# A mixture-of-experts stage with its first slots split earlier, its first gather by column halves, and its last expert pair and final norm written out

## What is computed

```python
h = h + memory_cross_attention(...)            # its last product is o @ w_xo ("xo1")
hn = rmsnorm(h, norm_ffn_g)
logits = hn @ w_router                         # 8 experts, the top 2 per token
y = zeros
for e in range(8):
    y = y + combine[:, e:e+1] * ((silu(hn @ w_gate[e]) * (hn @ w_up[e])) @ w_down[e])
out = rmsnorm(h + y, norm_final_g)             # D_EXPERT is 3584
```

## Time and profile before

| | us |
|---|---|
| median of three runs | 2310.11 |
| the profiled execution | 2310.16 |
| its span, first to last instruction | 2308.0 |
| PE busy / DVE busy / ACT busy | 2190.6 / 1751.8 / 1330.9 |
| expert stage, first slot's first matmul to its last | 1299.4 to 2288.9 |

### The profile page before, as it was taken

One profiled execution on the slowest core, in us unless ns is written; L12 is line 12 of the kernel. 1 busy time (PEld: TensorE's weight loads), 2 busy tenths in 40 slices (PEclk: granted clock), 3 DMA queues, 4 the chain that ended last, 5 costly groups with the idle time before them and its releaser, 6 DMA issues.

```text
span 2308.0 us, 34771 instructions
## 1 busy us (share of the span) xinstructions
PE 2190.6 (95%) x13807; PEld 1962.3 (85%) x13807; DVE 1751.8 (76%) x1928; ACT 1330.9 (58%) x1306; POOL 76.7 (3%) x160
## 2 busy tenths in 40 slices
PE   7999999999988899999898999999999999999997
PEld 4989988998978899999788888888888788888886
DVE  5768967874885455548865688888898888888887
ACT  3564435553534344435344677777777777777775
POOL 5002200000000000000000000000000000000000
PEclk8998999999999899999999999999999999999998
DMA  9636857655533346556334599999999999999994
GB/s 273 194 124 218 271 177 204 184 175 174 180 118 132 92 133 184 178 164 189 113 128 140 185 359 358 371 334 356 363 367 356 338 371 356 365 335 366 359 371 172
DMA packets 415931, 567.03 MB, mean 246 GB/s; under 512 B 17146, under 2 KB 268260, under 8 KB 415776
## 3 DMA queue, kind: packets, MB, share of 16 engines
q1 hardware_dynamic: 410736, 557.36, 71.3%
q0 software_dynamic: 5040, 7.41, 1.3%
HBM read 562.89 MB, written 1.84 MB: 245 GB/s over the span
## 4 chain that ended last, share of the span: by engine, by line
PE 81%; DVE 9%; ACT 3%; issue 2%; DVEq 0%; ACTq 0%
PE pair L1084 61%; PE misc L1084 13%; DVE arena L2000 3%; DVE wlo L1646 2%; PE misc L1559 1%; PE pair L1526 1%; DVE wlo L2206 1%; ACT whi L638 1%; PE misc L1154 1%; PE misc L1410 1%; PE misc L1138 0%; DVE opl L1664 0%; DVE rt L1671 0%; PE misc L1271 0%; ACT whi L1014 0%
## 5 line engine op out<-in xcount | busy, mean ns | idle before, releaser
L2206 DVE TENSOR_TENSOR wlo<-raw,whi 128x2048 fp32r<-128x2048 f32 x338 | 768.5, 2289 | 113.0 <-ACT whi L1014 111.8
L1014 ACT CAST whi<-raw 128x2048 fp32r<-128x2048 f32 x338 | 646.8, 1917 | 204.0 <-PE pair L1084 120.3
L1084 PE MATMUL pair<-hh,whi 128*128 128x256 f32 x1840 | 533.6, 290 | 23.2 <-DVE hl L1664 19.6
L1646 DVE TENSOR_TENSOR wlo<-raw,whi 128x2048 fp32r<-128x2048 f32 (+1 forms) x174 | 385.0, 2215 | 193.3 <-ACT whi L638 192.6
L1084 PE MATMUL pair<-hl,whi 128*128 128x256 f32 x1840 | 527.6, 287 | 0.0
L1084 PE MATMUL pair<-hh,wlo 128*128 128x256 f32 x1840 | 527.3, 287 | 0.0
L1084 PE MATMUL pair<-whi,oph 128*128 128x512 f32 (+1 forms) x1024 | 391.7, 383 | 5.7 <-DVE wlo L2206 3.9
L1084 PE MATMUL pair<-wlo,oph 128*128 128x512 f32 (+1 forms) x1024 | 386.1, 377 | 0.0
L1084 PE MATMUL pair<-whi,opl 128*128 128x512 f32 (+1 forms) x1024 | 385.9, 377 | 0.0
L1084 PEld LDWEIGHTS pair<-hh,whi 128*128 128x128 f32 x1840 | 360.8, 196 | 29.4 <-issue 25.6
L638 ACT CAST whi<-raw 128x2048 fp32r<-128x2048 f32 (+1 forms) x174 | 320.6, 1843 | 78.8 <-PE pair L1084 71.9
(11 more groups left out here) (437 smaller groups left out, 2480.1 us busy)
## 6 DMA issues: line engine op xcount, KB each, us to landing
raw<-in_moe_w_gate_dram SPq DMA_DIRECT2D x114, 1024.0 KB, 6.9
raw<-in_moe_w_up_dram SPq DMA_DIRECT2D x112, 1024.0 KB, 7.3
raw<-in_moe_w_down_dram SPq DMA_DIRECT2D x112, 1024.0 KB, 6.7
raw<-in_w_in_dram SPq DMA_DIRECT2D x38, 1024.0 KB, 5.7
raw<-in_w_mod_dram SPq DMA_DIRECT2D x24, 1024.0 KB, 5.7
raw<-in_w_up_dram SPq DMA_DIRECT2D x44, 512.0 KB, 5.1
raw<-in_w_xkv_dram SPq DMA_DIRECT2D x16, 1024.0 KB, 5.4
raw<-in_ffn_w_gate_dram SPq DMA_DIRECT2D x22, 512.0 KB, 3.9
```

The costliest lines, as they stand in the source:

```text
L1014: act.copy(whi[:, q, :], raw[:, r, :]).then_inc(sem("hi_ready"), 1)
L1084: ins = pe.matmul(out_, lhs, rhs, start=start and i == 0, stop=stop and i == 2)
L1646: dve.tensor_tensor(wlo[:, i_ % SPLIT, 0:size], raw[:, raw_of(n), 0:size], whi[:, i_ % SPLIT, 0:size].bitcast(F32), ALU.subtract).then_inc ...
L2206: dve.tensor_tensor(wlo[:, q, :], raw[:, r, :], whi[:, q, :].bitcast(F32), ALU.subtract).then_inc(sem("lo_ready"), 1)
```

## The change

- SP no longer loads the two slots of expert 0 at the end of a pass; the second pass loads them itself.
- `moe_hi(0, 0)` and `(0, 1)` stand in ACT's loop over the `xo1` groups, behind the squares of groups 1 and 2; `moe_lo(0, 0)` and `(0, 1)` stand behind DVE's `add_plain` of the same groups.
- The token parts are turned and split in the order 0, 2, 1, 3 (the first column half of both token blocks first). The first gather waits for two parts ahead of banks 0 and 1, and for four ahead of banks 2 and 3.
- The loops over expert pairs have three passes. The last pair follows as straight code, its last expert with `last=True`: no gather, no `placed`, no extra slots; in its last down slot the three products of both row chunks go to column half 0 first and then to half 1, and the output is weighed and split by halves.
- DVE loads the flag ahead of that split. It jumps over the second pass behind it, and only then does the four additions, each with its own signal.
- ACT loads the table of the root ahead of the sums, squares all four parts, sums the two column halves through the bias of the root, and scales token block 0; DVE multiplies block 0 with the gain beforehand and scales block 1.
- Parts are written out in the order 0, 2, 1, 3.

```diff
+LAST_PARTS = (0, 2, 1, 3)
+TOKEN_PARTS = (0, 2, 1, 3)
...
-                for k in (0, 1):
-                    load(NE - 1 + NE * p, 0, k + MOE_SLOTS)
...
+                load(NE, 0, 0)
+                load(NE, 0, 1)
                 moe_pass(1)
-            for q in range(4):
+            for n, q in enumerate(LAST_PARTS):
                 i, cols = q // 2, slice((q % 2) * 512, (q % 2 + 1) * 512)
-                sp.wait_ge(sem("fin_scaled"), q + 1)
+                if i == 0:
+                    sp.wait_ge(sem("x_copied"), 4 + 4 + n // 2 + 1)
+                else:
+                    sp.wait_ge(sem("fin_scaled"), n // 2 + 1)
...
+                if j in (1, 2):
+                    moe_hi(0, j - 1)
...
-            for q in range(4):
-                act.wait_ge(sem("hn_turned"), q + 1)
-                act.activation(hn_hi[:, q // 2, (q % 2) * 512:(q % 2 + 1) * 512], banks[:, q, :], ACT.Copy,
+            for n, q in enumerate(TOKEN_PARTS):
+                act.wait_ge(sem("hn_turned"), n + 1)
+                act.activation(hn_hi[:, q // 2, (q % 2) * 512:(q % 2 + 1) * 512], banks[:, n, :], ACT.Copy,
...
+                if last:
+                    upto(MOE_SLOTS - 1)
+                    act.wait_ge(sem("m_w"), E + 1)
+                    for m in range(2):
+                        if m == 0:
+                            act.wait_ge(sem("ranked"), 2 + p)
+                        else:
+                            act.wait_ge(sem("slot_used"), E * MOE_SLOTS + (n_split + MOE_SLOTS))
+                        act.activation(ye_hi[:, m * 512:(m + 1) * 512], misc[:, 2 + m, :], ACT.Copy, scale=weigh_slot[:])\
+                            .then_inc(sem("m_yc"), 1)
+                    return
...
+                with act.Fori(0, NE // 2 - 1) as i:
                     for u in range(2):
                         moe_expert(i, u, p)
-
-            moe_hi(0, 0)
-            moe_hi(0, 1)
+                for u in range(2):
+                    moe_expert(NE // 2 - 1, u, p, last=u == 1)
...
-            act.wait_ge(sem("moe_added"), 1)
-            act.activation(work[:, 0:4, :].rearrange("p a b -> p (a b)"), x_acc[:, 0], ACT.Square, accum_out=tiny[:, 6, 0:1])\
-                .then_inc(sem("fin_sq"), 1)
-            act.wait_ge(sem("fin_sq"), 2)
-            act.activation(token_root, tiny[:, 6, 0:2], ACT.Sqrt, bias=consts[:, 0:1], scale=1.0 / D).then_inc(sem("root_ready"), 1)
+            act.activation(tiny[:, 7, 2:3], consts[:, 0:1], ACT.Sqrt)
+            for n, q in enumerate(LAST_PARTS):
+                act.wait_ge(sem("moe_added"), n + 1)
+                act.activation(work[:, 2 * n:2 * n + 2, :].rearrange("p a b -> p (a b)"), x_acc[:, q // 2, (q % 2) * 512:(q % 2 + 1) * 512],
+                               ACT.Square, accum_out=tiny[:, 6, n:n + 1]).then_inc(sem("fin_sq"), 1)
+                if n == 1:
+                    act.wait_ge(sem("fin_sq"), 2)
+                    act.activation(tiny[:, 7, 0:2], tiny[:, 6, 0:2], ACT.Identity, bias=consts[:, 0:1], scale=1.0 / D)\
+                        .then_inc(sem("fin_sq"), 1)
+            act.wait_ge(sem("fin_sq"), 5)
+            for i in range(TB):
+                act.activation(token_root[:, i:i + 1], tiny[:, 6, 2 + i:3 + i], ACT.Sqrt, bias=tiny[:, 7, i:i + 1], scale=1.0 / D)\
+                    .then_inc(sem("root_ready"), 1)
+            act.wait_ge(sem("h_scaled"), DC * (NORM["ffn1"] + 1) + 3)
+            for m in range(2):
+                act.activation(x_acc[:, 0, m * 512:(m + 1) * 512], work[:, 4 * m:4 * m + 2, :].rearrange("p a b -> p (a b)"), ACT.Copy,
+                               scale=token_rs[:, 0:1]).then_inc(sem("x_copied"), 1)
...
-            for i in range(TB):
-                for c in range(DC):
-                    ins = pe.transpose(banks[:, 2 * i + c // 4, (c % 4) * P:(c % 4 + 1) * P], work[:, c, i * P:(i + 1) * P], ident[:])
-                    if c % 4 == 3:
-                        ins.then_inc(sem("hn_turned"), 1)
+            for n, q in enumerate(TOKEN_PARTS):
+                for c in range(4):
+                    cc, tok = 4 * (q % 2) + c, slice((q // 2) * P, (q // 2 + 1) * P)
+                    ins = pe.transpose(banks[:, n, c * P:(c + 1) * P], work[:, cc, tok], ident[:])
+                ins.then_inc(sem("hn_turned"), 1)
...
-            pe.wait_ge(sem("h_lo"), DC * NORM["ffn1"] + 4)
-
-            def gather(G):
+
+            def gather(G, first=False):
 
                 pe.wait_ge(sem("m_gt"), G + 1)
                 for b in range(4):
+                    if first:
+                        pe.wait_ge(sem("h_lo"), DC * NORM["ffn1"] + 2 * (b // 2) + 2)
...
+                        final = last and j == JE - 1 and half == 1
+                        for c, m in [(c, m) for m in range(2) for c in range(2)] if final else [(c, m) for c in range(2) for m in range(2)]:
                             x = slice((2 * half + c) * P, (2 * half + c + 1) * P)
-                            for m in range(2):
-                                col = slice(c * D + m * 512, c * D + (m + 1) * 512)
-                                ins = three(misc[:, 2 + m, :], whi[:, q, col], wlo[:, q, col], h_hi[j % 2][:, x], h_lo[j % 2][:, x],
-                                            j == 0 and half == 0 and c == 0, j == JE - 1 and half == 1 and c == 1, True)
+                            col = slice(c * D + m * 512, c * D + (m + 1) * 512)
+                            ins = three(misc[:, 2 + m, :], whi[:, q, col], wlo[:, q, col], h_hi[j % 2][:, x], h_lo[j % 2][:, x],
+                                        j == 0 and half == 0 and c == 0, j == JE - 1 and half == 1 and c == 1, True)
+                            if final and (c, m) == (1, 0):
+                                ins.then_inc(sem("ranked"), 1)
...
-                if u == 1:
+                if u == 1 and not last:
...
+                with pe.Fori(0, NE // 2 - 1) as i:
                     for u in range(2):
                         moe_expert(i, u, p)
-                pe.wait_ge(sem("m_xlo"), 4 * (NE // 2 + 1) * (p + 1))
-                for r in range(4):
-                    scatter(r, banks[:, r, :], 1, NE * (p + 1) + 1)
+                for u in range(2):
+                    moe_expert(NE // 2 - 1, u, p, last=u == 1)
+                pe.wait_ge(sem("m_c"), NE * (p + 1) + 1)
+                for n, r in enumerate(LAST_PARTS):
+                    scatter(r, banks[:, r, :], 1, (NE + 1) * (p + 1) + n // 2)
...
+                    if l == 1 and j in (1, 2):
+                        moe_lo(0, j - 1)
...
+            def last_added(p, signal):
+
+                for n, r in enumerate(LAST_PARTS):
+                    dve.wait_ge(sem("m_s"), 4 * (NE + 1) * p + (4 * NE + n + 1))
+                    part = x_acc[:, r // 2, (r % 2) * 512:(r % 2 + 1) * 512]
+                    dve.tensor_tensor(part, banks[:, r, :], part, ALU.add).then_inc(sem(signal), 1)
...
-                    if j == 5 and u == 1:
+                    if j == 5 and u == 1 and not last:
...
+                if last:
+                    upto(MOE_SLOTS - 1)
+                    if p == 0:
+                        dve.wait_ge(sem("overflow_known"), 1)
+                        st["over"] = dve.value_load(flag[0:1, 0:1], min_val=0, max_val=1)
+                    for m in range(2):
+                        cols = slice(m * 512, (m + 1) * 512)
+                        dve.wait_ge(sem("m_yc"), S + (2 + m))
+                        dve.scalar_tensor_tensor(ye_lo[:, cols], misc[:, 2 + m, :], weigh_slot[:], ye_hi[:, cols].bitcast(F32),
+                                                 ALU.mult, ALU.subtract).then_inc(sem("m_yl"), 1)
+                    return
...
             tokens_low(2)
             tokens_low(3)
-            moe_lo(0, 0)
...
-            moe_lo(0, 1)
             moe_pass(0)
-            over = dve.value_load(flag[0:1, 0:1], min_val=0, max_val=1)
-            with dve.If(over > 0):
+            with dve.If(st["over"] > 0):
+                last_added(0, "m_added")
                 moe_pass(1)
-                dve.wait_ge(sem("m_added"), 8 * (NE + 1) + 4)
-            dve.wait_ge(sem("m_added"), 4 * (NE + 1) + 4)
-            dve.memset(small[:, 1, 3:4], 0.0).then_inc(sem("moe_added"), 1)
-
-            dve.wait_ge(sem("moe_added"), 1)
-            dve.tensor_tensor_reduce(work[:, 4:8, :].rearrange("p a b -> p (a b)"), x_acc[:, 1], x_acc[:, 1], 1.0, 0.0, ALU.mult, ALU.add,
-                                     tiny[:, 6, 1:2]).then_inc(sem("fin_sq"), 1)
-            dve.wait_ge(sem("root_ready"), len(ROOTS) + 1)
-            link(dve.reciprocal(token_rs, token_root))
+                dve.wait_ge(sem("m_s"), 8 * (NE + 1))
+            last_added(0, "moe_added")
             dve.wait_ge(sem("router_landed"), 32)
-            for q in range(4):
-                i, cols = q // 2, slice((q % 2) * 512, (q % 2 + 1) * 512)
```

(58 more changed lines are left out.)

40 lines of the change are left out of this document (16 added, 24 removed).

## The result

Six runs of the changed kernel took 2283.1 to 2299.7 us, median 2287.57; six of the kernel before 2300.9 to 2312.5, median 2309.75. The ratio is 0.9921, 95% interval 0.990 to 0.9943. That is 22 us by the medians and 18 by the ratio, where 10.4 were forecast. So the sum of parts met the one execution that can be read, which is partly luck, and missed the level of the others. Both need an account.

A forecast was written before the change was run, and what follows sets the result against it. PE was taken as the bound, busy 245 of 248 us in each of four expert passes. Gains of 1.3 (start), 1.3 (last pair) and 7.8 (end) sum to 10.4, so 2310.16 becomes 2299.8 us; range 2294.8 to 2304.8.

The forecast's parts named there:

- the sum of parts: Whole kernel: 1.3 at the start, 1.3 for the last pair, 7.8 at the end; 10.4 us won, giving 2299.8 us.
- the level: Whole kernel: gains were subtracted from the profiled execution of 2310.16 us, 0.05 us above the median.
- The first gather's clock: Start of expert stage: gather starts 1.3 us earlier, still at half clock; bounds 0 to 4.2 us, 1.3 taken.
- rival B: More won: first gather keeps full clock (2.9 more) or ACT's jump costs nothing (1.3 more); both 2295.6 us; chance 0.22.
- Splitting early: Expert start: moving two casts and two differences ahead gives nothing more by itself; slot 2 stays next to be late.
- The last pair: Expert loop, last pair as straight code: one return goes, 1.3 us won; bounds 2.2 won and 1.8 lost.
- rival C: Less won: loop's exit costs PE a jump (3.1 less) or first gather's end stays (1.3 less); both 2304.2 us; chance 0.19.
- rival E: Slower: straight pair starves PE of instructions; 34 us lost if all 11 packets stall, time 2334 us; chance 0.04.
- The last gather: Before the last down product: dropping a 3.83 us gather for no pair exposes a 0.85 us wait; 3.0 us won.
- The tail: After the last down product: weighing by halves, earlier additions, norm and writes; end at 2300.2 for 2308.0, 7.8 won including the gather.
- hardest term: Tail: ACT's flag load (0.8) and jump (3.1) behind its last half, hidden before; bounds 0 and 3.9 us, all taken.
- rival D: Hardly any gain: queue order hides the tail's gains, such as a square awaiting a table; about 2307 us; chance 0.05.

The follow-up runs named there:

- the late gather: Changed kernel with token parts in the old order and the first gather waiting for all four, early split kept; median 2298.32 us, ratio 0.9956 against the kernel before.

## Why the prediction was wrong, and where it was right

**Where it failed: the level.** "The sum is made against the profiled execution, 0.05 us above the median" took the stages ahead of the change as fixed, and the range held only the bounds of the edited parts. But the same instructions reach the mark between 1269.2 and 1283.9 us in fourteen traces of all kernels, as the granted clock falls more or less often at PE's pauses. What the runs showed in place of a fixed level is one that moves by up to 17 us, beside a change of 11 us in the edited stretch, for which 10.4 were forecast. That the profiled execution came out 0.1 us from the forecast is luck: it was the slowest of its six. In the session of the result the changed kernel got 0.975 to 0.984. In the two others it got about 0.975 and 0.977, and its medians, 2296.0 and 2294.0, lie inside the range of 2294.8 to 2304.8 or 0.8 below. Why one session's clocks are higher wasn't found. By the ratios, two more sessions give 11 and 14 us where the first gave 18, so what lies above 11 isn't a fixed part of the change, but a small effect of it on the clock ahead of the mark isn't excluded. The level of a run of this kernel is open by 17 us, and the range should have had that on both sides.

**The first gather's clock (mis-sized).** "I take 1.3, since the row shows half clock from the first matmuls on" chose wrongly between its two ends. The start moved by 1.3 as worked out, and 2.65 more came at full clock, when PE's pause had shrunk from 2.0 to 0.7 us; the late gather put both back. This was the first half of rival B.

**Splitting early "gives nothing more by itself" (wrong as written).** It was priced against the slow gather. That much holds, as the late gather shows. With the short one, undoing it costs 6.2 us: slots 0 and 1, not slot 2, are late next. That it costs nothing in `xo1` held: the router products keep their spacing (17.8 us from the first to the last in both).

**The last pair.** One return less, 1.3 us forecast; the returns measured 1.3 to 2.9 us in all traces, so the gain depends on which one goes. The exit cost PE nothing to be seen, so rival C falls. The gain of one return was given back by the half clock behind the first one (1.35 us) in the pair of traces above. Code without returns gains 6 us more, and rival E was wrong at its root.

**The last gather.** 3.0 forecast, 2.5 measured; the wait for slot 40 came as predicted, 0.94 for 0.85.

**The tail.** Without the gather, 7.8 - 3.0 = 4.8 us were forecast, and 5.05 measured in the first pair of traces (19.35 to 14.3). The match is partly luck, since 1.5 us of the 19.35 are the scatters at half clock: against the second trace of the kernel before (17.85) the changed kernel's three traces (14.0 to 14.3) show only 3.6 to 3.9. Its hardest term, that ACT pays for a jump that the trace of before hid, was right: 3.55 us from the last weighing to the table load for 3.9. The rule on taken branches that was named from the Trainium skill (Runtime: NRT & Kernel Launch, Instruction fetch mechanics) agrees with 2.72 on ACT, in place of DVE's 3.09; that a fetch is what fills the time no experiment shows apart. The drain of 1380 ns behind a table load that the Trainium skill states (ScalarE: Activation LUTs, What ACT_TABLE_LOAD costs) doesn't show: the first square starts 1.5 us after the load began, 0.2 of it a root. No table was loaded among the squares, so rival D falls. What the sum didn't say is that the norm in pieces is worth only 0.6 to 0.9 of this. That the rest is the weighing by halves and the scatters under DVE's jump is argued from the timelines, not shown by an experiment.

**The sum.** 10.4 forecast. By the parts: 1.3 + 2.65 at the start, 5.05 in the tail, and from the first return on 3.8 for the last gather and one return, less 1.8 (0.5 for a longer first return, 1.35 for the pass at half clock behind it); 1.3 + 2.65 + 5.05 + 3.8 - 1.8 = 11.0, the stretch's difference. Two errors of opposite sign nearly cancelled. With the second trace of the kernel before the same sum has 1.5 less in the tail and 1.35 more at the third return.

## What to carry to other kernels

Before giving a range for a kernel whose engine pauses often, ask how far its granted clock moves between executions: compare runs at equal clock as long as the edit itself leaves the clock alone, and read the worth of an edit from the rows just around it, since returns and half clock elsewhere in the same stretch can hide it. A short wait ahead of a burst of matmuls can cost twice over, once as a wait and once as half clock behind it. A jump over code that doesn't run kept DVE waiting 2.77 and 3.09 us and ACT 2.45 to 2.72 here, 2.0 to 2.3 us of it in the kernel's time; put it where that engine waits anyway, with the short tail repeated in both arms, and write a loop of few long passes out straight where the engine that bounds it returns.

## What the runs showed that was not expected

- The same PE instructions ahead of the change took 1269.2 to 1283.9 us, and whole runs of one kernel 2296.5 to 2315.5, longer as the granted clock was lower (0.970 to 0.982).
- PE's first gather ran at full clock after a pause of 0.7 us (in eleven traces of eleven) and at half clock after 2.0 to 2.1 us (three of three). Behind a return of the loop it isn't so plain: half clock followed waits of 2.02, 2.07, 2.33, 2.58, 2.65 and 2.90 us, but not those of 2.12, 2.22 and 2.49 us in experiments and of 2.22 and 2.66 us in the kernel before. Behind the last difference of the kernel before, a wait of 3.00 us gave half clock and one of 3.09 full clock. So the pause's length alone doesn't decide it, at the gather perhaps neither; what does stays open.
- A return of the loop with some 1,100 matmuls in it cost PE 1.3 to 2.9 us, differently each time (24 returns in eleven traces), while straight code of four times the length cost nothing.
